# Hybrid decoder layer on one core: heads 4 to 7 of RWKV-7 take the two 64-token chunks of a turn in exchanged places

## What is computed

```python
def rwkv7_step(state, inp):
    r, w, k, v, a, b = inp
    sa = jnp.einsum('bhvk,bhk->bhv', state, a)
    state = state * w[:, :, None, :] + sa[..., None] * b[:, :, None, :] + v[..., None] * k[:, :, None, :]
    y = jnp.einsum('bhvk,bhk->bhv', state, r)
    return state, y
```

## Time and profile before

| | |
|---|---|
| median of 3 runs | 1014.44 us (1013.91 to 1015.71) |
| the profiled execution | 1015.55 us |
| its span in the profile | 1013.8 us |
| PE busy | 987.9 us, 97% |
| DVE, ACT, POOL busy | 503.4, 371.7, 433.3 us |
| mean granted TensorE clock | 0.994 |

### The profile page before, as it was taken

How to read it: one execution, slowest core, us unless ns; L and a number is a source line. 1 busy time by engine, 2 the same in 40 slices (tenths; PEclk the granted TensorE clock), 3 DMA queues, 4 the chain that set the end, 5 groups by cost and what they waited for, 6 DMA issues and landing times.

```text
span 1013.8 us, 14170 instructions
## 1 busy us (share of the span) xinstructions
PE 987.9 (97%) x5774; PEld 805.2 (79%) x5774; DVE 503.4 (50%) x634; ACT 371.7 (37%) x462; POOL 433.3 (43%) x346
## 2 busy tenths in 40 slices
PE   6999999999999999999999999999999999999996
PEld 5887878788877878788777777878888888888885
DVE  5846865645474546684854656853343343310004
ACT  5414414532352264134653432642342332221112
POOL 4864421532344116224223563455455455454350
PEclk9999999999999999999998999999999999999998
DMA  8223312341333254319126455323333332322312
GB/s 279 95 86 123 125 64 83 107 142 64 104 108 104 85 178 171 105 67 315 56 84 208 166 185 168 84 83 83 109 98 83 108 99 83 113 94 87 121 42 83
DMA packets 107650, 117.69 MB, mean 116 GB/s; under 512 B 2768, under 2 KB 86736, under 8 KB 107600
## 3 DMA queue, kind: packets, MB, share of 16 engines
q1 hardware_dynamic: 99680, 100.70, 31.1%
q10 hardware_dynamic: 7920, 16.25, 4.1%
HBM read 100.70 MB, written 16.25 MB: 115 GB/s over the span
## 4 chain that ended last, share of the span: by engine, by line
PE 75%; issue 13%; POOL 7%; DVE 2%; DMA 1%; ACT 1%; SPq 1%; ACTq 0%; POOLq 0%; DVEq 0%
PE ps L1590 26%; PE ps L1488 13%; PE ps L1489 13%; PE ps L1490 13%; POOL w_lo L575 7%; PE ps L1654 2%; DMA w_raw<-w_in 1%; PE ps L1635 1%; PE ps L1697 1%; PE ps L1688 1%; PE ps L1681 1%; PE ps L1693 1%; PE ps L1678 1%; PE ps L1625 1%; DVE row L978 1%
## 5 line engine op out<-in xcount | busy, mean ns | idle before, releaser
L575 POOL TENSOR_TENSOR w_lo<-w_raw,w_hi 128x512 fp32r<-128x512 f32 x296 | 408.8, 1411 | 540.6 <-ACT w_hi L663 540.3
L663 ACT CAST w_hi<-w_raw 128x2048 fp32r<-128x2048 f32 x75 | 142.9, 1905 | 165.4 <-PE ps L1490 150.7
L1488 PE MATMUL ps<-a_hi,w_hi 128*128 128x512 f32 (+1 forms) x416 | 159.2, 383 | 1.3 <-DVE a_lo L1412 1.0
L1489 PE MATMUL ps<-a_lo,w_hi 128*128 128x512 f32 (+1 forms) x416 | 158.4, 381 | 0.0
L1490 PE MATMUL ps<-a_hi,w_lo 128*128 128x512 f32 (+1 forms) x416 | 158.4, 381 | 0.0
L1590 PE MATMUL ps<-a_hi,w_hi 128*128 128x512 f32 x384 | 154.0, 401 | 0.0
L1590 PE MATMUL ps<-a_lo,w_hi 128*128 128x512 f32 x384 | 153.6, 400 | 0.0
L1590 PE MATMUL ps<-a_hi,w_lo 128*128 128x512 f32 x384 | 151.7, 395 | 0.0
L1488 PEld LDWEIGHTS ps<-a_hi,w_hi 128*128 128x128 f32 x416 | 78.2, 188 | 18.0 <-DVE a_lo L1412 1.8
L1490 PEld LDWEIGHTS ps<-a_hi,w_lo 128*128 128x128 f32 x416 | 78.2, 188 | 15.1
L1489 PEld LDWEIGHTS ps<-a_lo,w_hi 128*128 128x128 f32 x416 | 78.2, 188 | 14.7
(11 more groups left out here) (314 smaller groups left out, 1535.8 us busy)
## 6 DMA issues: line engine op xcount, KB each, us to landing
w_raw<-w_in SPq DMA_DIRECT2D x33, 1024.0 KB, 5.2
w_raw<-w_ffn_in SPq DMA_DIRECT2D x44, 512.0 KB, 4.8
spill<-spill_buf ACTq DMA_DIRECT2D x27, 512.0 KB, 3.2
w_raw<-w_ffn_out SPq DMA_DIRECT2D x11, 1024.0 KB, 4.8
w_raw<-w_branch SPq DMA_DIRECT2D x5, 1024.0 KB, 8.1
g_ab<-spill SPq DMA_DIRECT2D x8, 512.0 KB, 5.1
w_raw<-w_out SPq DMA_DIRECT2D x4, 1024.0 KB, 5.0
proj<-spill SPq DMA_DIRECT2D x1, 3072.0 KB, 15.1
```

The lines of the kernel that those rows point to most:

```text
L575: g.tensor_tensor(w_lo[:, b, c], w_raw[:, b, c], w_hi[:, b, c].bitcast(F), ALU.subtract).then_inc(lo_ready, 1)
L663: s.copy(w_hi[:, b], w_raw[:, b]).then_inc(hi_ready, 1)
L1488: t_.matmul(dst, w0, a0, start=first, stop=False)
L1489: t_.matmul(dst, w0, a1, start=False, stop=False)
```

## The change

For heads 4 to 7 the tokens of a turn stand in exchanged halves: what was on rows 0 to 63 is on rows 64 to 127, and the other way round. `at(h, c)` gives the half in which head h has chunk c. In the loop over c, heads 0 to 3 then use one tile of the array and heads 4 to 7 another, and `HEADS` takes them in turn (0, 4, 1, 5, ...), at L1681, L1688 and L1697. The products at L1688 go to banks 1 and 3. The products at L1678 and L1693 stay 128x128 and the number of products is the same; L1678 now starts both banks 4 and 5 in each chunk.

To get there and back, tokens are exchanged where they are read: `mix_tokens`, the sum of `sig`, the copies of `g_tok` and of `y_a` are split. The copies of `xs` and `uv` are split in two, since a chunk now lies on both halves. DVE waits once, for the second `y_done`, before it sums `y`. The order of steps is otherwise what it was, and so are all counts of fill steps.

```diff
@@ -358,6 +358,8 @@
         TILES = [((i + NH // 2 * half) % NH, half) for i in range(NH) for half in range(2)]
         MT_PAIRS = [(0, 2), (1, 3), (4, 6), (5, 7)]
         mt_bank = lambda h: (1, 2, 3, 1)[[h in pair for pair in MT_PAIRS].index(True)]
+        at = lambda h, c: c if h < NH // 2 else 1 - c
+        HEADS = [h for pair in zip(range(NH // 2), range(NH // 2, NH)) for h in pair]
         own = [slice(HD * c, HD * c + HD) for c in range(2)]
         other = [own[1], own[0]]
 
@@ -763,7 +765,11 @@
                 need(z_ready)
                 s.activation(sig[:], sig[:], ACT.Sigmoid).then_inc(sig_ready.sem, 1)
                 need(g_done)
-                s.copy(g_tok[:], ps[:, 2].rearrange("p (h c) -> p h c", h=NH)).then_inc(g_ready.sem, 1)
+                g_ps = ps[:, 2].rearrange("p (h c) -> p h c", h=NH)
+                s.copy(g_tok[:, 0:NH // 2], g_ps[:, 0:NH // 2])
+                for b in range(2):
+                    last = s.copy(g_tok[own[b], NH // 2:NH], g_ps[other[b], NH // 2:NH])
+                last.then_inc(g_ready.sem, 1)
                 need(ssq_ready)
                 s.activation(sq[:], sq[:], ACT.Sqrt).then_inc(norm_ready.sem, 1)
                 if T > 0:
@@ -791,11 +797,17 @@
                     last = s.copy(by_bank(wt[r, :, HD // 2:HD]), ps[r, 1:4:2, 0:P].rearrange("p a (h t) -> p a h t", h=NH // 2))
                 last.then_inc(w_ready.sem, 1)
                 for c in range(2):
-                    r = other[c]
+                    parts = [(at(h0, c), slice(h0, h0 + NH // 2)) for h0 in (0, NH // 2)]
                     need(x_done, c)
-                    s.copy(xs[r], ps[r, 4 + c].rearrange("p (h v) -> p h v", h=NH)).then_inc(x_ready.sem, 1)
+                    for b, hs in parts:
+                        r = other[b]
+                        last = s.copy(xs[r, hs], ps[r, 4 + b].rearrange("p (h v) -> p h v", h=NH)[:, hs])
+                    last.then_inc(x_ready.sem, 1)
                     need(u_done, c)
-                    s.copy(uv[r, c], ps[r, 1].rearrange("p (h v) -> p h v", h=NH)).then_inc(u_ready.sem, 1)
+                    for b, hs in parts:
+                        r = other[b]
+                        last = s.copy(uv[r, b, hs], ps[r, 1 + 2 * (hs.start // 4)].rearrange("p (h v) -> p h v", h=NH)[:, hs])
+                    last.then_inc(u_ready.sem, 1)
                     if c == 0:
                         evacuate(7)
                 evacuate(8)
@@ -809,8 +821,12 @@
                 evacuate(10)
                 evacuate(11)
                 need(y_turned)
-                dst = y_a[:].rearrange("p j (t c) -> p j t c", c=P)
-                s.copy(dst[:, :, T], ps[:, 5].rearrange("p (j c) -> p j c", j=NJ)).then_inc(y_a_ready.sem, 1)
+                dst = y_a[:].rearrange("p j (t c) -> p j t c", c=P)[:, :, T]
+                src = ps[:, 5].rearrange("p (j c) -> p j c", j=NJ)
+                s.copy(dst[:, 0:NJ // 2], src[:, 0:NJ // 2])
+                for b in range(2):
+                    last = s.copy(dst[:, NJ // 2:NJ, own[b]], src[:, NJ // 2:NJ, other[b]])
+                last.then_inc(y_a_ready.sem, 1)
                 if T == NT - 1:
                     next_high(T, PER_T - 1)
 
@@ -1014,16 +1030,32 @@
                 k = slice(2 * i, 2 * i + 2)
                 v.tensor_tensor(a_lo[:, k], x_ct[:, k], a_hi[:, k].bitcast(F), ALU.subtract).then_inc(a_lo_ready, 1)
 
-            MIXED_AFTER = {N_UNSCALED: (0, 6), N_UNSCALED + 1: (6, RT - 2), N_RWKV - 1: (RT - 2, RT)}
+            MIXED_AFTER = {N_UNSCALED: (0, 2 * NJ), N_UNSCALED + 1: (2 * NJ, 3 * NJ), N_RWKV - 1: (3 * NJ, RT)}
 
             def mix_tokens(T, j0, j1):
 
-                js = slice(j0, j1)
-                now = proj[:, js, PAD:PITCH].rearrange("p j (t c) -> p j t c", c=P)[:, :, T]
-                before = proj[:, js, PAD - 1:PITCH - 1].rearrange("p j (t c) -> p j t c", c=P)[:, :, T]
-                link(v.tensor_tensor(xm[:, js], before, now, ALU.subtract))
+                js, j3 = slice(j0, j1), min(j1, 3 * NJ)
+
+                def shifted(lo, b0, b1):
+
+                    c = lo + T * P
+                    return proj[:, j0:j3, c + HD * b0:c + HD * b1].rearrange("p (q two j) t -> p q two j t", two=2, j=NJ // 2)
+
+                parts = []
+                if j3 > j0:
+                    to = xm[:, j0:j3].rearrange("p (q two j) t -> p q two j t", two=2, j=NJ // 2)
+                    parts.append((to[:, :, 0], [shifted(lo, 0, 2)[:, :, 0] for lo in (PAD - 1, PAD)]))
+                    for b in range(2):
+                        parts.append((to[:, :, 1, :, HD * b:HD * b + HD], [shifted(lo, 1 - b, 2 - b)[:, :, 1] for lo in (PAD - 1, PAD)]))
+                if j1 > j3:
+                    parts.append((xm[:, j3:j1], [proj[:, j3:j1, lo + T * P:lo + T * P + P] for lo in (PAD - 1, PAD)]))
+                for dst, (before, now) in parts:
+                    last = v.tensor_tensor(dst, before, now, ALU.subtract)
+                link(last)
                 link(v.tensor_tensor(xm[:, js], xm[:, js], over(params[:, C_MU + j0:C_MU + j1], (P, j1 - j0, P)), ALU.mult))
-                return v.tensor_tensor(xm[:, js], xm[:, js], now, ALU.add)
+                for dst, (before, now) in parts:
+                    last = v.tensor_tensor(dst, dst, now, ALU.add)
+                return last
 
             slope = [2.0 ** (-8.0 * (a + 1) / (HG * NG)) for a in range(HG * NG)]
 
@@ -1131,8 +1163,14 @@
                 need(xm_ready)
                 v.tensor_tensor(kk[:], k_, par(C_KK), ALU.mult).then_inc(kk_ready.sem, 1)
                 need(z_done)
-                v.tensor_tensor(sig[:, 0], ps[:, 0].rearrange("p (j t) -> p j t", j=NJ), par(C_W0), ALU.add)
-                v.tensor_tensor(sig[:, 1], ps[:, 1].rearrange("p (j t) -> p j t", j=NJ), par(C_A0), ALU.add).then_inc(z_ready.sem, 1)
+                z = ps[:, 0:2].rearrange("p a (j t) -> p a j t", j=NJ)
+                base = params[:, C_W0:C_W0 + 2 * NJ].rearrange("p (a j) -> p a j", a=2).unsqueeze(3)
+                low_j, high_j = slice(0, NJ // 2), slice(NJ // 2, NJ)
+                v.tensor_tensor(sig[:, :, low_j], z[:, :, low_j], base[:, :, low_j].broadcast_to((P, 2, NJ // 2, P)), ALU.add)
+                for b in range(2):
+                    last = v.tensor_tensor(sig[:, :, high_j, own[b]], z[:, :, high_j, other[b]],
+                                           base[:, :, high_j].broadcast_to((P, 2, NJ // 2, HD)), ALU.add)
+                last.then_inc(z_ready.sem, 1)
                 need(ssq_done)
                 need(sq_ready)
                 v.tensor_scalar(sq[:], ps[:, 3].rearrange("p (j t) -> p j t", j=NJ), 1e-12, None, ALU.max).then_inc(ssq_ready.sem, 1)
@@ -1160,9 +1198,10 @@
 
                 ends = ep[:].rearrange("p j (c t) -> p c j t", t=HD)[:, :, :, HD - 1:HD]
                 for c in range(2):
-                    v.tensor_tensor(small[:, 64 + 8 * c:72 + 8 * c].rearrange("p (j h) -> p j h", h=2),
-                                    ends[:, c].broadcast_to((P, NJ, 2)),
-                                    head_ones[:, ::HD].unsqueeze(1).broadcast_to((P, NJ, 2)), ALU.mult)
+                    to = small[:, 64 + 8 * c:72 + 8 * c].rearrange("p (j h) -> p j h", h=2)
+                    for j, js in ((0, low_j), (NJ // 2, high_j)):
+                        v.tensor_tensor(to[:, js], ends[:, at(2 * j, c), js].broadcast_to((P, NJ // 2, 2)),
+                                        head_ones[:, ::HD].unsqueeze(1).broadcast_to((P, NJ // 2, 2)), ALU.mult)
                 link(v.tensor_tensor(rk[:], r_, k2[:], ALU.mult))
                 v.tensor_tensor(rk[:], rk[:], par(C_RK), ALU.mult).then_inc(rk_ready.sem, 1)
                 link(v.tensor_copy(tt[:], ident_pair[:].unsqueeze(1).broadcast_to((P, NH, HD))))
@@ -1236,8 +1275,8 @@
 
                 y_ps = [ps[own[c], 4 + c].rearrange("p (h v) -> p h v", h=NH) for c in range(2)]
                 full = (P, NH, HD)
+                need(y_done, 1)
                 for c in range(2):
-                    need(y_done, c)
                     last = v.tensor_reduce(small[own[c], 40:40 + NH], y_ps[c], AX, ALU.add)
                 link(last)
                 link(v.tensor_scalar(small[:, 40:40 + NH], small[:, 40:40 + NH], 1.0 / HD, None, ALU.mult))
@@ -1667,7 +1706,6 @@
                 fill_steps(6)
                 need(w_ready)
                 for c in range(2):
-                    r, ru = own[c], other[c]
                     if c > 0:
                         need(s_ready, c - 1)
                     elif T > 0:
@@ -1675,26 +1713,32 @@
 
 
                     for j in range(NJ):
-                        t_.matmul(ps[:, 4 + c, j * P:(j + 1) * P], ar[:, j, c * P:(c + 1) * P],
-                                  state[:, j].rearrange("p h v -> p (h v)"), start=(j == 0), stop=False, skip_group_check=True)
-                    for h in range(NH):
```

(25 more changed lines are left out.)

## The result

| | before | after |
|---|---|---|
| median of 4 runs | 1015.06 us (1013.91 to 1015.71) | 1005.25 us (1003.70 to 1006.91) |
| ratio, with its 95% interval | 1 | 0.9909 [0.9895, 0.9922] |
| profiled execution | 1015.55 us, span 1013.8 | 1004.86 us, span 1003.1 |
| mean granted clock, share of full speed | 0.994 | 0.996 |

The change saves 9.8 us by the medians, 9.2 by the ratio and 10.7 between the two profiled executions. Forecast were 1006.6 us, a gain of 7.8 (both against the median of the three runs shown, 1014.44).

What follows compares the result with a forecast made beforehand. TensorE, busy 97% of the span, was taken to bound the kernel. Terms -11.1 + 0.5 + 1.7 + 0.6 + 0.45 = -7.8 us, from the 1014.44 us median, gave 1006.6 us, range 1004.0 to 1010.6.

Steps and rivals of the forecast that it cites:

- 24 groups: L1681, L1688, L1697 over two chunks and four turns: paired records save 0.46 us a group, -11.1 us.
- `x_ready` where ACT is free: Fifth fill step, chunk 0 in four turns and chunk 1 in the first: 0.10 us late each, +0.5 us.
- `x_ready` behind the cast: Chunk 1 of the other three turns, `xs` starting as the `w_hi` cast ends: 0.56 us late each, +1.7 us.
- `u_ready`: Wait gating L1693: split `uv` copies arrive 0.08 us late, eight times, +0.6 us.
- `y_a`: Three copies instead of one on ACT ahead of `sq`: 0.15 us at three turn boundaries, +0.45 us.
- `g_tok`, first turn: Split `g_tok` copies were expected to disappear in gaps, costing nothing.
- rival without overlap: Accumulating products served one after another, nothing gained and copies still paid: 1016.3 us, or 1017.7; chance 0.06.
- the one in which column halves don't pair: Eight groups at L1697 give nothing at 64 moving columns: 1010.3 us; chance 0.04.
- rival with copies at 1.0: Split copies on ACT take 1.0 us instead of 0.74, lengthening 16 waits by 4.2 us: 1010.8 us; chance 0.08.
- the lateness is hidden: Split pair as fast as the whole copy, only the cast and `y_a` cost: 1005.0 us; chance 0.10.
- `s_ready`: Chunk 0 state result gating L1678's weight load: in time with 0.08 us left, no cost.

Runs made afterwards that it cites:

- small copies: The changed kernel with a one-element ACT copy ahead of each `xs` and `uv` copy: 1008.84 us, ratio 0.9947 to the kernel before.
- head order: The changed kernel with heads taken 0 to 7 in each group, all splits kept: 1011.14 us, ratio 0.9962 to the kernel before.
- three and three: The changed kernel with heads in the order 0, 1, 2, 4, 5, 6, 3, 7: 1008.80 us in one run.
- two and two: The changed kernel with heads in the order 0, 1, 4, 5, 2, 3, 6, 7: 1007.94 us, ratio 0.9915 to the kernel before.

## Why the prediction was right, step by step

The forecast of 1006.6 us lies 1.35 above the measured median of 1005.25, inside its range and on the right side. The gain of the turns as measured, 9.04, would have given 1005.4. Three of its terms were too high by 0.4 to 0.6 us, and one priced at nothing wasn't nothing.

| term, us | forecast | trace of after |
|---|---|---|
| 24 groups | -11.1 | -11.05 |
| `x_ready` where ACT is free | +0.5 | 0 |
| `x_ready` behind the cast | +1.7 | +1.3 |
| `u_ready` | +0.6 | 0 |
| `y_a` | +0.45 | +0.4 |
| `g_tok`, first turn | 0 | +0.3 |
| sum of the turns | -7.8 | -9.04 |
| stretch at half clock | none | -1.6, in the profiled executions |

**The pairs.** L1722, L1730 and L1741 take 0.61 each in the chain, and inside them two records start 5 to 8 ns apart and the next pair 50 to 53 behind, 0.058 for two. 0.46 a group, as forecast. The rival without overlap and the one in which column halves don't pair are out: L1741 pairs like the others. The Trainium skill, TensorEngine Tiling (Array Packing), Instruction Overhead, gives each matmul about 60 cycles and advises against taking the tiling factor from a dimension that is already small. The trace does not contradict the figure: 0.058 us for two records of 64 columns are 70 cycles a record at 2.4 GHz, the clock granted here, and half of what the same record takes on one tile. Nor does the advice reach this change, whose products keep their 64 moving columns; the prediction read more out of it than it says.

**The copies.** Two of 64 x 256 take 0.75 on ACT (rows `x2` above), as L791 had it, so the rival with copies at 1.0 is out. The Trainium skill, same page, PSUM Bottleneck, says that tiling speeds up TensorE but not the copies out of PSUM; the trace agrees in that 0.75 stands for 0.58. The Trainium skill says there only that the copy may become the bottleneck, after a fourfold speedup; that by it this rival was the likely one was my reading. At this size the split of `xs` and `uv` costs nothing, except where `xs` stands behind the cast.

**`x_ready` where ACT is free, and `u_ready`,** are the step that failed: 1.1 us were priced and nothing was paid. It counted lateness from the first moment at which the weight load behind the wait may begin. The weight loads of PE in after:
```profile
240.76 0.19 PEld L1629 LDWEIGHTS ps<-a_hi,w_lo 128*128 128x128 f32 x1
241.10 0.19 PEld L1629 LDWEIGHTS ps<-a_hi,w_hi 128*128 128x128 f32 x1 [0.16 <-ACT xs L804]
```
and the products of the same steps:
```profile
240.99 0.39 PE L1629 MATMUL ps<-a_hi,w_lo 128*128 128x512 f32 x1
241.22 0.40 PE L1629 MATMUL ps<-a_hi,w_hi 128*128 128x512 f32 x1
241.54 0.68 PE L1730 MATMUL ps<-xs,wt 64*64 64x64 f32 x16
```
The load could have begun with the product at 240.99 and began at 241.10, 0.1 late as forecast; its product is in step all the same, 0.23 behind the one before. A product can start 0.11 after its weight load (241.22 - 241.10), where it usually has 0.23 (240.99 - 240.76); the 0.12 between is cover that I had left out. It is used up to the last hundredth, as the small copies show. Ahead of L1736, where PE waits for `uv`, it is the same:
```profile
243.07 0.42 PEld L1736 LDWEIGHTS ps<-uv,bk_tok 128*128 128x128 f32 x3 [0.16 <-ACT uv L809]
```
This load could have begun with the product at 242.95, 0.12 before, and L1736 starts at 243.19, 0.24 behind that product and so in step. In all eight places it comes 0.10 to 0.12 late and nothing is paid. So the lateness is hidden, as in the rival of that name, but not by a faster copy, the ground on which I had given it 0.10; its value of 1005.0 is nearest to the result.

**`x_ready` behind the cast** went as described: `xs` starts at 248.21 as the cast ends, its product 0.56 behind the fourth instead of 0.23, and L1730 another 0.10 late, together 0.43 for a forecast 0.56, less by the same 0.12. Moving the cast gave back 0.39 to 0.42 in each of the three turns.

**`y_a`** occupies ACT for 0.59 (275.02 to 275.61) instead of 0.49, and the wait for `sq` is 0.53 instead of 0.41: 0.12 at each of three boundaries for a forecast 0.15. The estimate from overlapping copies on the same partitions was right and the margin on top of it not needed.

**`g_tok`** was costed at nothing, with the gaps of ACT and DVE in a full turn as cover. In the first turn that cover is missing: the copies stand ahead of a table load, a root and an eviction for which TensorE waits. 0.27 us at 102.40, 0.36 by the end of that stretch, 0.34 by the run that moves them.

**`s_ready`**, the thinnest cover, held: L1717's first weight load, behind five fill steps, isn't late in any turn, and no wait behind L1270 and L1272 is in the list.

**The other 1.6** between the two profiles is clock, and no run shows it to be the change's. Length of the stretch at half clock behind the four-row products, by profile: before 6.8 and 6.8 us, after 3.4 and none; in the experiments, in their order here, 3.4, 3.4, 3.4, 6.8, 3.4, 3.4, none, 3.4. It varies between executions of one program, and costs half its length. Both kernels have runs with a mean granted clock from 0.992 to 0.998; the average is 0.9948 over 31 runs of before and 0.9955 over 6 of after, which is some 0.7 us. By the ratios the change is worth 9.2 and 9.5 us in the two comparisons, close to the 9.0 of the turns, with intervals of 1.4 and 1.9 us to either side. Whether the changed programs have the stretch shorter on average (nine profiles with 3.4 or none and one with 6.8, against two with 6.8) stays open.

## What to carry to other kernels

- Small products that follow each other on one tile start 0.058 us apart here, and pairs on two tiles take the same 0.058 for two (1.07 us a group and 0.61): let neighbours go to different row or column halves, or at least put no more than two products of one tile in a row (0.66); in the program that is a reordering of a loop and an exchange of places. Then look at who produced and who reads the exchanged places: the copies that have to be split are where the gain leaks.
- Before costing a late operand, ask what the consumer overlaps ahead of its own start. Here a weight load may come 0.12 us late for nothing, and each 0.1 beyond it is paid at once.
- If a gain leaves a result standing behind unrelated work on its engine (a cast, a copy whose reader comes later), move that work behind it: three such moves took the gain of the turns from 9.0 us to 12.2 (9.8 to 13.4 by the medians).

## What was not expected of the hardware

- A record for a free tile starts while three earlier ones for a busy tile are still waiting: 0.89 us for a group in head order, 0.78 with three and three, 0.66 with two and two, 0.61 alternating, 1.07 on one tile.
- Two copies on ACT of 128 partitions overlap by 0.10 us (275.02 + 0.37 = 275.39, the next starts at 275.29), while `xs`'s two, on different 64 partitions, don't (248.30 + 0.27 to 248.57, then 248.58, and 0.37 each).
- A weight load and its product can be 0.11 us apart; in a run of fill products they are 0.23 apart.
- The granted clock falls to 0.50 for 3.4 or 6.8 us, or not at all, behind eight products with weights on four rows that start 0.43 us apart (0.53 the first two), in executions of the same program.
